# Second attention's head norms: norm factors in four buffers that their store frees, a semaphore for each wide buffer, and the turned key part laid into each head by transfers

## The reference, cut to what matters

```python
q = (rmsnorm(q_lat, q_norm_g) @ w_uq).reshape(B, S, N_HEADS_MLA, QK_HEAD_DIM)          # 8 heads of 96
kv = (rmsnorm(kv_lat, kv_norm_g) @ w_ukv).reshape(B, S, N_HEADS_MLA, QK_NOPE_DIM + V_HEAD_DIM)
k_nope, v = split_cols(kv, (QK_NOPE_DIM, V_HEAD_DIM))                                   # 64 and 64
k_rope = jnp.broadcast_to(k_pe[:, :, None, :], (B, S, N_HEADS_MLA, QK_ROPE_DIM))        # 32, one for all heads
k = jnp.concatenate([k_nope, k_rope], axis=-1)
q = rope_tail(rmsnorm(q, q_head_g), cos, sin)
k = rope_tail(rmsnorm(k, k_head_g), cos, sin)
o_attn = blocked_bidirectional_attention(q, k, v) * jax.nn.silu(g_attn)
```

## Time and profile before

| | |
|---|---|
| time, median of 3 runs | 2526.86 us (2525.43 to 2527.62) |
| time of the profiled execution | 2529.12 us |
| its span in the trace | 2527.3 us |
| PE busy | 2407.3 us, 95% of the span |
| DVE busy | 1345.9 us, 53% |
| ACT busy | 936.5 us, 37% |
| POOL busy | 968.6 us, 38% |
| granted TensorE clock, mean | 0.986 of full speed |
| wide loads of this stage | 16, of 512 KB |

### The profile page before, as it was taken

How to read it: one execution, slowest core, us unless ns; L and a number is a source line. 1 busy time by engine, 2 the same in 40 slices (tenths; PEclk the granted TensorE clock), 3 DMA queues, 4 the chain that set the end, 5 groups by cost and what they waited for, 6 DMA issues and landing times.

```text
span 2527.3 us, 34014 instructions
## 1 busy us (share of the span) xinstructions
PE 2407.3 (95%) x13374; PEld 1965.2 (78%) x13374; DVE 1345.9 (53%) x1566; ACT 936.5 (37%) x1541; POOL 968.6 (38%) x574
## 2 busy tenths in 40 slices
PE   6999888899999999999999899998999999999999
PEld 3788767677878888888877578877888888888877
DVE  3799678767732223222584977854410246454342
ACT  4301267625343234422554477752410111323220
POOL 1444300032255444544433310026134444787643
PEclk9999989999999999999999899999999999999999
DMA  6111266321121111111122300002011111111132
GB/s 268 42 42 57 83 186 184 114 88 45 43 63 51 42 55 62 56 34 55 54 109 67 143 25 2 1 26 84 18 50 50 42 50 51 66 52 43 50 125 92
DMA packets 66080, 175.12 MB, mean 69 GB/s; under 512 B 6724, under 2 KB 25416, under 8 KB 64392
## 3 DMA queue, kind: packets, MB, share of 16 engines
q1 hardware_dynamic: 59936, 149.66, 18.1%
q10 hardware_dynamic: 5992, 23.34, 2.4%
HBM read 161.89 MB, written 11.08 MB: 68 GB/s over the span
## 4 chain that ended last, share of the span: by engine, by line
PE 83%; DVE 10%; ACT 3%; issue 2%; DMA 1%; POOL 1%; SPq 0%; ACTq 0%; DVEq 0%; POOLq 0%
PE region L300 15%; PE region L302 15%; PE region L301 15%; PE region L2545 3%; PE region L2547 3%; PE region L2546 3%; PE aux L2545 3%; PE aux L2547 3%; PE aux L2546 3%; PE pv L2109 2%; PE aux L2099 2%; PE pv L300 2%; PE pv L301 2%; PE pv L302 2%; DVE conv L1164 1%
## 5 line engine op out<-in xcount | busy, mean ns | idle before, releaser
L3006 POOL TENSOR_TENSOR w_hi<-w_raw,der 128x1024 fp32r<-128x1024 f32 x96 | 192.3, 2003 | 889.8 <-PE region L302 834.8
L300 PE MATMUL region<-h_hi,w_hi 128*128 128x512 f32 x928 | 367.2, 396 | 10.6 <-issue 5.0
L301 PE MATMUL region<-h_lo,w_hi 128*128 128x512 f32 x928 | 364.4, 393 | 0.0
L302 PE MATMUL region<-h_hi,w_lo 128*128 128x512 f32 x928 | 363.7, 392 | 0.0
L2582 POOL TENSOR_TENSOR w_lo<-w_raw,w_hi 128x512 fp32r<-128x512 f32 x153 | 199.4, 1311 | 241.6 <-ACT w_hi L296 239.7
L3009 POOL TENSOR_TENSOR w_lo<-w_raw,w_hi 128x1024 fp32r<-128x1024 f32 x96 | 261.2, 2721 | 7.5
L300 PEld LDWEIGHTS region<-h_hi,w_hi 128*128 128x128 f32 x928 | 176.0, 190 | 54.9 <-issue 8.8
L302 PEld LDWEIGHTS region<-h_hi,w_lo 128*128 128x128 f32 x928 | 176.1, 190 | 37.3
L301 PEld LDWEIGHTS region<-h_lo,w_hi 128*128 128x128 f32 x928 | 176.1, 190 | 35.7
L296 ACT ACTIVATE w_hi<-w_raw 128x512 fp32r<-128x512 f32 (+1 forms) x159 | 100.2, 642 | 256.9 <-PE pv L302 85.1
L1164 DVE SCALAR_TENSOR_TENSOR conv<-glu,par,conv 128x1024 f32<-128x1024 f32 x120 | 188.2, 1568 | 3.4
(11 more groups left out here) (481 smaller groups left out, 5884.8 us busy)
## 6 DMA issues: line engine op xcount, KB each, us to landing
w_raw<-units SPq DMA_DIRECT2D x122, 512.0 KB, 3.5
w_raw<-units SPq DMA_DIRECT2D x77, 256.0 KB, 2.6
w_raw<-w_ada_late SPq DMA_DIRECT2D x32, 512.0 KB, 4.3
bias<-na_bias SPq DMA_DIRECT2D x24, 384.0 KB, 4.0
w_slot<-units SPq DMA_DIRECT2D x35, 256.0 KB, 2.6
ada_buf<-w_ada SPq DMA_DIRECT2D x4, 2048.0 KB, 28.8
head_wide<-v_spill SPq DMA_DIRECT2D x16, 512.0 KB, 3.7
x_sb<-x_t ACTq DMA_DIRECT2D x2, 2048.0 KB, 14.1
```

The costliest lines, as they stand in the source:

```text
L300: pe.matmul(dst, wh, xh, start=first, stop=False)
L301: pe.matmul(dst, wh, xl, start=False, stop=False)
L302: return pe.matmul(dst, wl, xh, start=False, stop=last)
L3006: pool.tensor_tensor(w_hi[:, s], w_raw[:, s], one_col.broadcast_to([P, 1024]), ALU.mult)\
```

## The change

Three edits in `Heads`, and what follows from them.

1. The factors lie in four buffers (`head_factors`, in place of the two of `head_scale`), and `root(h)` waits for the landing of the 4 KB store of head h - 4, no longer for the landing of the wide load of head h - 2. SP's wait for a free wide buffer stands between the store and the load instead of ahead of the store.
2. Each of the three wide buffers has a semaphore of its own.
3. The key heads' second multiply on DVE is gone. The turned part is left unscaled in `tmp[RR, 1]`, and SP copies it into rows 64 to 127 of each key head by a transfer (64 partitions of 4 KB, 256 KB) right behind that head's wide load, on the same semaphore. The one multiply left covers all 128 rows, with a gain of 1 for rows 64 to 127. `k_last` makes ACT wait, ahead of head 14, until the eight query heads are finished, since that head's place in `k_h` is the query table's.

```diff
         elif step == 4:
-            ch(e.tensor_tensor(k_turned[r], k_turned[r], tmp[r, 1], ALU.add))
+            ch(e.tensor_tensor(tmp[r, 1], k_turned[r], tmp[r, 1], ALU.add))
...
         def spread_sp(self, e, h):
             reach(e, f"{self.tag}_rs", h + 1)
+            line = v_spill[0, 8 * h:8 * h + 8]
+            e.dma_start(line, self.scale_at[0:P:16, h % 4]).then_inc(sem("wide_st"), 16)
             if h >= 3:
                 reach(e, f"{self.tag}_sc", h - 2)
-            line = v_spill[0, 8 * h:8 * h + 8]
-            e.dma_start(line, self.scale_at[0:P:16, h % 2, 0:P]).then_inc(sem("wide_st"), 16)
             reach(e, "wide_st", 16 * (h + 1))
-            e.dma_start(self.wide[h % 3][:], line.rearrange("a c -> (a c)").partition_broadcast(P)).then_inc(sem(f"wide_ld{h % 2}"), 16)
+            e.dma_start(self.wide[h % 3][:], line.rearrange("a c -> (a c)").partition_broadcast(P)).then_inc(sem(f"wide_ld{h % 3}"), 16)
 
         def reach_wide(self, e, h):
-            reach(e, f"wide_ld{h % 2}", 16 * (h // 2 + 1))
+            moved = len([k for k in range(HEADS, h + 1) if k % 3 == h % 3])
+            reach(e, f"wide_ld{h % 3}", 16 * (h // 3 + 1 + moved))
...
-                if h >= 2:
-                    if self.wide:
-                        self.reach_wide(e, h - 2)
-                    elif self.heads[h - 2].packed:
+                if self.wide:
+                    if h >= 4:
+                        reach(e, "wide_st", 16 * (h - 3))
+                elif h >= 2:
+                    if self.heads[h - 2].packed:
...
     def k_finish(e, ch, dst, rs):
-        scaled(sp_("kh"), NOPE)(e, ch, dst, rs)
-        ch(e.tensor_tensor(dst[RR], k_turned[RR], rs[RR], ALU.mult))
+        scaled(sp_("kh"))(e, ch, dst, rs)
+
+    def k_last(e, h):
+        reach(e, "hd_sc", HEADS)
...
             for h in range(2 * HEADS):
                 qk_heads.spread_sp(sp, h)
+                if h >= HEADS:
+                    sp.dma_start(k_h[RR, h - HEADS], tmp[RR, 1]).then_inc(sem(f"wide_ld{h % 3}"), 16)
                 if h in (2, 4, 6, 8, 11, 14):
```

More of the change, by code:

```diff
@@ L1892, in __init__, with factors @@
             self.tag, self.heads, self.scale_at, self.wide = tag, heads, scale, wide
+        def factors(self, h):
+            return self.scale_at[:, h % 4] if self.wide else self.scale_at[:, h % 2]
         def spread_sp(self, e, h):
             reach(e, f"{self.tag}_rs", h + 1)
+            line = v_spill[0, 8 * h:8 * h + 8]
+            e.dma_start(line, self.scale_at[0:P:16, h % 4]).then_inc(sem("wide_st"), 16)
             if h >= 3:
                 reach(e, f"{self.tag}_sc", h - 2)
-            line = v_spill[0, 8 * h:8 * h + 8]
-            e.dma_start(line, self.scale_at[0:P:16, h % 2, 0:P]).then_inc(sem("wide_st"), 16)
             reach(e, "wide_st", 16 * (h + 1))
-            e.dma_start(self.wide[h % 3][:], line.rearrange("a c -> (a c)").partition_broadcast(P)).then_inc(sem(f"wide_ld{h % 2}"), 16)
+            e.dma_start(self.wide[h % 3][:], line.rearrange("a c -> (a c)").partition_broadcast(P)).then_inc(sem(f"wide_ld{h % 3}"), 16)
         def reach_wide(self, e, h):
-            reach(e, f"wide_ld{h % 2}", 16 * (h // 2 + 1))
+            moved = len([k for k in range(HEADS, h + 1) if k % 3 == h % 3])
+            reach(e, f"wide_ld{h % 3}", 16 * (h // 3 + 1 + moved))
         def pe(self, e, pos, meanwhile=None):
@@ L1966, in root @@
                 n = P if self.wide else QTR
-                root_act(e, tag, self.scale_at[:, h % 2, 0:n], aux[:, bank:bank + n], self.heads[h].rows, eps_col)
+                root_act(e, tag, self.factors(h), aux[:, bank:bank + n], self.heads[h].rows, eps_col)
             for h, head in enumerate(self.heads):
@@ L2003, in dve @@
                 pos.next_use()
-                inverse_dve(e, tag, h + 1, self.scale_at[:, h % 2, 0:P if self.wide else QTR])
+                inverse_dve(e, tag, h + 1, self.factors(h))
                 if h >= late:
@@ L2031, in build @@
     head_scale = fixed("head_scale", [2, QTR], 24 * KIB)
+    head_factors = fixed("head_factors", [4, P], 24 * KIB)
     qk_heads = Heads("hd", [
@@ L2037, in build @@
              k_h[:, h], k_finish, ready=(lambda e, k: reach(e, "nk_lo", k + 1)) if h == 0 else None,
-             before=k_before if h < 2 else None) for h in range(HEADS)
-    ], head_scale, wide=[place(f"head_wide{n}", [T], at) for n, at in enumerate([168, 172, 140])])
+             before=k_before if h < 2 else k_last if h == HEADS - 2 else None) for h in range(HEADS)
+    ], head_factors, wide=[place(f"head_wide{n}", [T], at) for n, at in enumerate([168, 172, 140])])
     def uv_pe(e, pos):
@@ L3291, in _small @@
         "qh": rows(np.concatenate([qh, qh[80:96], qh[64:80]])),
-        "kh": rows(kh),
+        "kh": rows(np.concatenate([kh[:NOPE], np.ones(P - NOPE, np.float32)])),
         "khr": rows(np.concatenate([np.zeros(NOPE, np.float32), kh[NOPE:], kh[NOPE:]])),
```

## The result

The changed kernel takes 2539.02 us (median of 5 runs, 2538.3 to 2541.3) against 2527.23 us before (5 runs): a ratio of 1.0046, 95% interval 1.0035 to 1.0057. It is slower by 11.8 us, twice the 5.7 us that the sum gave. That lies 0.5 us inside the upper end of the whole range (2522.5 to 2539.5), and above the range that was given for the forecast by itself (2528.5 to 2537).

What follows compares the result with a forecast made beforehand. DVE's row was taken as the bound, passing to the wide loads with the copies: the attention starts 4.3 us later, plus 1.4 us of PE's clock, 5.7 us on 2526.86 gives 2532.6 us; range 2522.5 to 2539.5, the forecast's own 2528.5 to 2537.

Steps and rivals of the forecast that it cites:

- The bound and the mechanism: DVE's row bounds heads 3 to 14 before the change; with the copies, the wide loads become the bound.
- the much slower rival: Reads and writes share half the partitions: a copy takes 2.4 us, 8.4 us more, 2541.0 us; chance 0.10.
- The row of the waits: ACT's 20.8 us of waits for wide loads go, but lie beneath DVE's row, so worth nothing by itself.
- the clock: After PE's longer wait the first six score matmuls run at 1.2 GHz: 1.4 us, bounds 0 and 2.8.
- The sign that ACT's roots wait for nothing: Listed as showing the forecast right: in the changed kernel's trace ACT's roots wait for no transfers.
- The steps of the loads: In the key heads, 4.6 us from one wide load to the next, six loads from head 10: 27.6 us.
- The last landing: The last head's wide load with the copy behind it lands 4.6 us after issue, before the multiply.
- The weight units: Units issued behind heads 11 and 14 stand ahead of the next store, 1.5 us each, 3.0 us together.
- The way the queue was put: On SP's queue a store waits for what was put ahead of it, so copies delay store and next load.
- The store that isn't held up: Faster rival: the 4 KB store passes the copy, low part starts 6.4 us sooner, 2521.9 us; chance 0.17.
- The copy in the gaps: No-change rival: copies fill idle DMA engine time, loads 4.0 us apart, 2527.3 us; chance 0.15.
- a copy of 0.6 us: If a copy reached all 16 DMA ports, taking 0.6 us not 1.2, the sum ends within 1 us of no change.

Runs made afterwards that it cites:

- e2: Changed kernel with each copy issued behind the next head's store instead of ahead of it; 2531.51 us, ratio 1.0019 to the kernel before.
- e1: Changed kernel without copies and with the key heads' second multiply back on DVE, leaving edits to waits and semaphores; 2529.95 us, 1.0012 to before.
- e6: Changed kernel with 70 more matmuls on PE ahead of the attention's scores, results unread; 2538.68 us, 1.0039 to before.
- e4: Changed kernel with the turned part stored to memory once and all eight copies read from there; 2541.69 us, 1.0064 to before.
- e7: Changed kernel with the two weight units behind heads 11 and 14 issued behind the last head's copy; 2534.49 us, 1.0030 to before.
- e5: Changed kernel with the eight copies issued from ACT on its own queue, one head behind ACT's work; 2536.78 us, 1.0033 to before.
- e3: Changed kernel with ACT copying the turned part into each key head in place of a transfer; 2528.00 us, 1.0004 to before.
- e11: Same kernel as e8, measured again over 11 runs; 2523.71 us, 0.9983 to before.
- e10: Kernel before with only the weight units behind heads 11 and 14 issued behind the last head; 2528.55 us, 1.0002 to before.
- e8: e3 with the two late weight units and 20 matmuls with unread results ahead of the scores; 2525.59 us, 0.9992 to before.

## Why the prediction was right and where it was short

**The bound and the mechanism held.** DVE's row was the bound before, ACT's waits lay beneath it, and with the copies the wide loads became the bound. The waits, the load steps and e2 show it.

**The time lies in the stated range by luck.** The loss was put at 5.7 us and is 11.8. The upper end of 2539.5 came from the much slower rival, in which a copy costs 2.4 us, and not from the forecast's own terms; the measured 2539.02 is outside the range that these were given. The chances had "slower" and "same" nearly even, 0.45 to 0.44.

**The row of the waits** held for the stage: e1's is 0.7 us longer than before. But the text had ACT's edit at nothing and the clock as a term of the whole; e1 shows that the clock's 1.3 us belong to this edit, and come without any copy. The sign that ACT's roots wait for nothing failed as well: two of them waited 5.0 us together for stores, which now land later, but DVE took their reciprocals more than 10 us after that, so it cost nothing.

**The steps of the loads** were the term that was mis-sized. I took 4.6 us; the four steps without a weight unit are 5.32, 4.92, 4.84 and 5.62 us, 5.2 us in the mean, which makes 3.5 us over six. In e6, with the same code in the stage, they are 4.9 us in the mean, so part of the 0.6 us is this execution. Two parts of the error can be named. The 4.6 us were taken from between 4.75 and 4.5, and the lower end was a misreading: at heads 6 and 7 the store was issued late, 3.04 us behind the load, because DVE was late, and then it landed in 1.82 us, hardly later than an undisturbed one, so the earlier trace rows shows next to no hold-up. And a copy holds the engines for 1.5 us and not 1.2. From memory it is 1.2 us (e4); whether that is because source and destination are the same 64 rows, or because the source is a tile at all, was not tried. With 4.75 us and 0.3 us for the copy a step is 5.05 us.

**The last landing** was mis-sized too: from the last load's issue (1459.77) to the multiply (1466.15) it took 6.4 us, not 4.6: 1.8 us. I had added the copy's engine time to the load's landing; the copy's own landing took 5.6 us in the median from its issue (the changed kernel's tile view of `k_h`):

```profile
DMA to landing us min/median/max: 5.3/5.6/6.0
```

**The weight units** cost 3.1 us by e7 against 3.0; by the two long steps of the changed kernel it is 3.5. **The clock** cost 1.3 us against 1.4. The sum of the stage: 4.23 (the prediction's 4.3 with less rounding) + 3.45 (the steps) + 0.46 (the two longer steps) + 1.78 (the last landing) + 0.29 (head 9's load, that much later from the start of the stage) = 10.2 us, which is what was measured.

**The way the queue was put was wrong.** The prediction spoke of what stands ahead on SP's queue. e5 shows that the queue does not matter, the engines do; the sum would have been the same.

**The rivals.** The store that isn't held up is ruled out by the changed kernel's own rows. Its price was also too high: e3, in which no copy holds a store, gains 2.6 us in the stage and not 6.4, since a load of 512 KB holds the next store as well once it is issued right behind the load, and POOL's split of the value weights, now earlier, delays DVE by 1.6 us ahead of head 10. The copy in the gaps is ruled out by the same rows: with a copy in each step the engines were busy for 0.63 of it, less than the 0.73 of the earlier trace rows, and the steps grew. What the idle part is made of, about 2 us in each step, no view of these runs shows. The prediction's remark that a copy of 0.6 us would bring the sum within 1 us of no change holds only without the clock's term (0.1 us; 1.5 us with it). The double price of a copy (2.4 us) was nearer in its time, 2541.0, than in its cause: the copy costs 1.5 us, and its total came near only because the last landing was long as well.

## What to carry to other kernels

A small transfer whose landing something waits for pays for the bytes that the DMA engines still have in hand from before it, on whichever queue; issue it ahead of the bulk that can wait (e2: 7.9 us of the stage for a different order of issue). Before moving work from a compute engine to transfers, see what waits for landings in the same loop; an engine with idle time beside it, here ACT, was a better place than the transfers (e3), though only with the late weight units and the idle matmuls did it beat the kernel before (e11, 4.3 us). And a wait that is taken off a side engine can gather into one wait ahead of the next stage, where PE's clock is then low when it counts (e1).

## What the runs showed of the hardware that I had not expected

- A copy between the same 64 rows of two tiles landed 5.6 us after its issue behind a 512 KB load, later than the 4 KB store issued behind it: copy at 1430.95, store at 1431.50, the store had landed by 1435.50, and the multiply that waited for the copy started at 1436.41.
- 256 KB into 64 partitions held the 16 engines for 1.5 us from a tile in the same 64 rows and 1.2 us from memory, by estimates that take off 1.38 us for the wide load beside it (512 KB over all partitions). Which property of the source makes the difference isn't shown.
- In a loop of store, landing and load, a step took the engine time of what was given in it and about 2 us more: 3.33, 4.07, 4.92 and 5.09 us for 512, 640, 768 and 1024 KB, with 1.7, 2.05, 2.9 and 2.92 us of engine time.
- In each kernel whose PE waited from 8.35 to 18.04 us ahead of the scores, the scores ran at the slow level (0.50 in the changed kernel's window), and the attention then took 1.1 to 1.4 us longer (221.0 or 221.1 against 219.7 and 219.9; e5, with 221.5, took 1.8 us longer than before, of which the rest isn't explained). In e11, behind a wait of 2.83 us, the drop came among the scores and cost nearly as much (220.9); behind waits of 0.71 to 2.23 us (e10, e8, e6, before) there was none.
